# Order of work in a two-transformer kernel: output projections by chunks inside the attentions, rotations at another place, last pieces by halves, another order at the head

## What is computed

```python
def first_block(x, ...):
    for i in range(2):
        h = x @ w_in[i]                       # q, k, v, index heads, u, vs
        a_out = dsa_attention(q, k, v, qi, ki, wi)     # 64 selected keys a query
        b_out = spatial_gating(gelu(u), gelu(vs), ...)
        mix = concatenate([a_out, b_out]) @ w_o[i]
        x = layer_norm(ALPHA * x + mix, ...)
        ffn = (silu(gate) * up) @ w_ffn_out[i]         # gate, up = x @ w_ffn_in[i]
        ple = (p[i] @ w_ple[i]) * sigmoid(x @ w_ple_gate[i])
        x = layer_norm(ALPHA * x + ffn + ple, ...)

def second_block(x, c, ...):
    cond = silu(c)
    for layer in range(2):
        sh1, sc1, g1, sh2, sc2, g2 = split(cond @ ada_w[layer] + ada_b[layer], 6)
        h = modulate(rms_norm(x), sh1, sc1)
        # layer 0: latent attention and a dilated one; layer 1: differential and block attention
        y = (even_mixer if layer == 0 else odd_mixer)(h, ...)   # ends in "@ w_out"
        x = x + g1 * y
        h = modulate(rms_norm(x), sh2, sc2)
        x = x + g2 * squared_relu(h @ mlp_w1[layer]) @ mlp_w2[layer]
    return x
```

## Time and profile before

| | us |
|---|---|
| three executions | 1358.96, 1360.89, 1361.48 |
| the profiled execution | 1359.15 |
| its span | 1357.3 |
| PE busy | 1301.2 |
| DVE busy | 919.9 |
| ACT busy | 654.1 |

### The profile page before, as it was taken

How to read it: one execution, slowest core, us unless ns; L and a number is a source line. 1 busy time by engine, 2 the same in 40 slices (tenths; PEclk the granted TensorE clock), 3 DMA queues, 4 the chain that set the end, 5 groups by cost and what they waited for, 6 DMA issues and landing times.

```text
span 1357.3 us, 16066 instructions
## 1 busy us (share of the span) xinstructions
PE 1301.2 (96%) x6436; PEld 1073.8 (79%) x6467; DVE 919.9 (68%) x1233; ACT 654.1 (48%) x882; POOL 114.4 (8%) x145
## 2 busy tenths in 40 slices
PE   5999999999899999999998999999999978999998
PEld 5877888887787788888698977888887767888886
DVE  4867777765695877775769856857667875644444
ACT  4653544443463544444465555544446544644542
POOL 2001000000000100000225200000004410000000
PEclk8999999999999999999999999999999989999999
DMA  9515587774451668886263304876754421445550
GB/s 371 219 48 186 221 312 308 310 304 148 186 179 63 218 247 310 310 310 233 82 202 125 127 1 165 330 282 261 291 222 184 155 94 39 179 175 182 174 182 31
DMA packets 40362, 270.36 MB, mean 199 GB/s; under 512 B 4560, under 2 KB 4560, under 8 KB 12000
## 3 DMA queue, kind: packets, MB, share of 16 engines
q1 hardware_dynamic: 37712, 259.31, 51.6%
q0 software_dynamic: 2432, 8.98, 1.8%
q10 hardware_dynamic: 144, 1.05, 0.2%
HBM read 268.27 MB, written 1.05 MB: 198 GB/s over the span
## 4 chain that ended last, share of the span: by engine, by line
PE 83%; DVE 10%; ACT 2%; issue 2%; DMA 1%; POOL 1%; SPq 0%; DVEq 0%; ACTq 0%; POOLq 0%
PE ps L1468 48%; PE ps L1458 24%; PE ps L1482 5%; DVE WB L1776 3%; PE ps L1442 2%; PE ps L1567 2%; PE ps L1543 1%; DMA RAW<-W 1%; ACT E L1580 1%; DVE st L2052 1%; ACT WB L1580 1%; DVE st L1980 1%; POOL st L1390 0%; DVE st L2129 0%; DVE X L2097 0%
## 5 line engine op out<-in xcount | busy, mean ns | idle before, releaser
L1776 DVE TENSOR_TENSOR WB<-RAW,WB 128x2048 fp32r<-128x2048 f32 (+4 forms) x210 | 453.5, 2162 | 271.5 <-ACT WB L1580 270.8
L1580 ACT ACTIVATE WB<-RAW 128x2048 fp32r<-128x2048 f32 (+4 forms) x210 | 379.9, 1810 | 210.5 <-PE ps L1468 199.6
L1458 PE MATMUL ps<-WB,XTH 128*128 128x512 f32 (+3 forms) x1176 | 314.4, 389 | 13.0 <-ACT XTH L1580 13.0
L1468 PE MATMUL ps<-WB,XTH 128*128 128x512 f32 (+3 forms) x1176 | 304.6, 381 | 3.4 <-DVE WB L1776 3.3
L1468 PE MATMUL ps<-WB,XTL 128*128 128x512 f32 (+3 forms) x1176 | 304.0, 380 | 1.1 <-DVE XTL L1781 1.1
L1458 PEld LDWEIGHTS ps<-WB,XTH 128*128 128x128 f32 x1176 | 215.0, 190 | 49.2 <-ACT XTH L1580 13.4
L1468 PEld LDWEIGHTS ps<-WB,XTH 128*128 128x128 f32 x1176 | 219.1, 190 | 43.5 <-DVE WB L1776 5.5
L1468 PEld LDWEIGHTS ps<-WB,XTL 128*128 128x128 f32 x1176 | 219.1, 190 | 39.5 <-DVE XTL L1781 1.3
L1458 PE MATMUL ps<-WB,HTH 128*128 128x512 f32 (+1 forms) x452 | 124.4, 396 | 0.5 <-ACT HTH L1580 0.5
L1468 PE MATMUL ps<-WB,HTH 128*128 128x512 f32 (+1 forms) x452 | 123.9, 395 | 0.0
L1468 PE MATMUL ps<-WB,HTL 128*128 128x512 f32 (+1 forms) x452 | 123.8, 394 | 0.0
(11 more groups left out here) (173 smaller groups left out, 964.8 us busy)
## 6 DMA issues: line engine op xcount, KB each, us to landing
RAW<-W SPq DMA_DIRECT2D x220, 1024.0 KB, 4.9
RAW<-W SPq DMA_DIRECT2D x22, 768.0 KB, 4.3
VEC<-vecd POOLq DMA_DIRECT2D x10, 512.0 KB, 7.7
RAW<-W SPq DMA_DIRECT2D x8, 512.0 KB, 3.4
RAW<-W SPq DMA_DIRECT2D x4, 648.0 KB, 5.3
RAW<-W SPq DMA_DIRECT2D x4, 576.0 KB, 3.9
GB<-xTd ACTq DMA_DIRECT2D x1, 1024.0 KB, 7.4
X<-xd SPq DMA_DIRECT2D x1, 1024.0 KB, 17.5
```

Of the source, the lines that this page charges most:

```text
L1458: eng.matmul(banks[b][:, 0:cw], x2[j][0], hi[:, j, c0:c0 + cw], start=first and j == 0, stop=False)
L1468: op = eng.matmul(banks[b][:, 0:cw], x2[j][0 if low_w else 1], (lo if low_w else hi)[:, j, c0:c0 + cw], start=False, stop=last and end and ...
L1580: return eng.activation(dst, src, f, **k)
L1776: eng.tensor_tensor(WB[:, it["raw"], 0:w], RAW[:, it["raw"], 0:w], WB[:, it["high"], 0:w].bitcast(F32), ALU.subtract).then_inc(*up("wl", n))
```

## The change

Eleven bf16 products and a memset are added, twelve padding products taken away, and some steps cut into smaller ones; all else is the same work in another order.

- **Head.** `xT` comes as three transfers (four quarters of the split `x0`), the constants in two, of which the larger part and the small vectors are asked for only after the input is split; the first chunk's items hold 2, 3 and 3 blocks (`FIRST`) instead of 4 and 4; the load of `x` comes four loads later; eleven products on a constant of ones (`warm`) stand at the very start of TensorE's queue; the `silu` of `cond` moves behind the sine and cosine.
- **Output projections.** `linear_k` does the first chunk by items: the blocks that are ready early for both t inside the attention, the others when their block of `MIX` is normalised, with four (or two) transposes directly ahead of their products. The guard and its flag go.
- **Attention.** `between[k]` puts the rotations after scores(k), so between VectorE's maxima and the step that needs the exponentials. Low parts are put down only in steps k < n-2, no longer in the last ones.
- **Halves.** `partial` does t's last products by column halves c, and `last(t, c, done)` is called for each; the last results are stored as four transfers of 128x512.
- **Layer 0 to 1 of the first block.** `mid_at=2` puts the transposes of t = 1 behind the first item of the second chunk; the two `rope_sel` steps stand together.

```diff
+FIRST = [(0, 2), (2, 3), (5, 3)]
...
+        def linear_k(name, lhs, evac, ready, turned=False):
+            its = chunk_items(name)
+            w, g, ps = its[0]["w"], uid(), [take(), take()]
+            advance()
+            its = its[::-1] if turned else its
+            for it in its:
+                for t in range(2):
+                    yield from ready(it["a"], t)
+                    b, fr = ps[t]
+                    lows([it])
+                    do("mm", it, t, "x", [(b, 0, w, (g, t) if it is its[-1] else None)], it is its[0], it is its[-1],
+                       wanted(lhs[t], "x", it), fr if it is its[0] else [], 0, it is its[-1], t)
...
                 old = list(low)
+                if k < len(between):
+                    for f in between[k]:
+                        f()
                 if 1 <= k <= n:
                     turns(units[k - 1], pads[k - 1] if k <= len(pads) else 2)
...
-                lows(old)
+                if k < n - 2:
+                    lows(old)
                 if k >= 2:
                     values(units[k - 2])
             cur["lag"] = False
-            lows()
...
-        loads(3)
-        do("load_x")
+        do("warm", free[0][0])
+        loads(2)
+        do("load_x1")
+        do("x0", 0, 0)
         advance(1)
-        xt_w = [[("xl0", t)] for t in range(2)]
-        do("x0", 0)
+        do("x0", 0, 4)
+        advance(1)
+        do("x0", 1, 0)
+        do("x0", 1, 4)
         advance()
-        do("x0", 1)
-        do("setup")
+        do("load_rest")
...
+            def ready(a, t):
+                if a == 0:
+                    while "out" not in keys_[t]:
+                        yield
+                    mo[t].extend(to_XT(MIX, 4, [keys_[t]["out"]], t, pad=3 if t else 0))
+
             def out_start():
-                while "out" not in keys_[0]:
-                    yield
-                mo[0][:] = to_XT(MIX, 8, [keys_[0]["out"], sgo], 0)
+                for t in range(2):
+                    mo[t].extend(to_XT(MIX, 8, [sgo], t, base=4))
                 yield
-                yield from linear("w_o", "x", mo, put_o(0), touter=True, guard=lambda: tail["go"], pad=(0, 3),
-                                  mid=lambda: mo[1].extend(to_XT(MIX, 8, [keys_[1]["out"], sgo], 1, pad=3)))
+                yield from linear_k("w_o", mo, put_o(0), ready, turned=True)
...
-            def last(t, done):
-                for c in range(2):
-                    do("add_out", (i, t, c), t, c, acc4[t][c][0], [done[c]] + x_o[t])
-                    give(acc4[t][c][0], ("add_out", (i, t, c)))
+            def last(t, c, done):
+                do("add_out", (i, t, c), t, c, acc4[t][c][0], [done] + x_o[t])
+                give(acc4[t][c][0], ("add_out", (i, t, c)))
+                if c == 0:
+                    return
...
-                fill = lined(part((2, 5)), [
-                    None, [ch[3, 1][1], ch[4, 1][0]], None,
-                    [ch[4, 0][1]], None,
-                    [ch[4, 1][1]], None,
-                    [lambda: turn_qk(3, 0, 8, twm), lambda: turn_qk(3, 1, 8, twm)],
-                    [lambda: turn_qk(4, 0, 12, twm), lambda: turn_qk(4, 1, 12, twm)]])
+                ch[4, 1][0]()
+                fill = part((2, 5))
+                between = [[ch[3, 1][1]], [ch[4, 0][1]], [ch[4, 1][1]],
+                           [lambda: turn_qk(3, 0, 8, twm), lambda: turn_qk(3, 1, 8, twm)],
+                           [lambda: turn_qk(4, 0, 12, twm), lambda: turn_qk(4, 1, 12, twm)]]
...
+            def warm(b):
+                on.wait_ge(*at("ones", 0))
+                for _ in range(11):
+                    op = eng.matmul(banks[b][:, :], cstb[:, 0:128], cstb[:, 128:640], start=True, stop=True)
+                op.then_inc(*up("warm", 0))
```

190 lines of the change are left out of this document (112 added, 78 removed).

## The result

| | before | after |
|---|---|---|
| median | 1360.83 us (5 executions) | 1354.49 us (5 executions, 1351.83 to 1356.18) |
| ratio | | 0.9946, 95% interval 0.9925 to 0.9966 |
| the profiled execution | 1359.15 us | 1356.18 us |
| its span | 1357.3 us | 1354.4 us |

A forecast was written before the change was run, and what follows sets the result against it. TensorE, busy 1301.2 of 1357.3 us, was taken as the bound, so only its waits and half-clock work could shrink. Terms -5.7, -0.56, -1.65, -3.55, -1.1, -0.6, -1.9 sum to -15.1: from 1359.15 to 1344.0 us, range 1336 to 1353.

The forecast's parts named there:

- Head: Start of the kernel: smaller first transfers let TensorE start at 6.3 instead of 9.69; -5.7 us, bounds -3 and -9.
- rival (c): Head's data come late, with more, smaller transfers in flight on three queues: head -3, total 1346.8 us; chance 0.10.
- rival (d): Clock stays at 1.2 GHz through the head: 1356.4 us, chance 0.06; uncovered copies drop it too: 1363, chance 0.06.
- First block's attentions: First block's two attentions: shorter wait for the low part, against uncovered copies to `XTH`; -0.28 us each, -0.56 for both.
- step 3: Second block's even layer: shorter waits for exponentials and `MIX`, copies to `XTH` uncovered once; -1.65 us, bounds -3 and 0.
- a wait for `XTH` above 1.5: Sign that the prediction is wrong; waits of 0.6 to 0.9 for `XTH` were expected at the ends of attentions.
- Odd layer, first attention: Rotations moved between maxima and `differ` bring E 3.5 earlier, where TensorE waited 6.86; -5.2 us.
- Odd layer, second attention: Low parts between first maxima +2.3 us, two uncovered `XTH` copies +1.15, low part ahead of the last reciprocal gone -1.8.
- step 4: Odd layer, both attentions: rotations, low parts, `XTH` copies and last reciprocal together; net -3.55 us, bounds -7 and 0.
- Boundaries: Layer 0 to 1 of the first block -1.1 us; layer 1 to second block -0.6, from the hidden half residual add.
- End: Kernel's end: 1.37 instead of 2.74 of VectorE behind the last product, smaller last store; -1.9 us, bounds -1.3 and -2.2.
- Rival (b): Attentions give nothing, each new wait eating what the old one gives back; 2 to 4 fall to 0: 1349.9 us; chance 0.20.

The follow-up runs named there:

- e8: e1's kernel without the eleven products on ones at the start of TensorE's queue: 1347.25 us.
- e3: Changed kernel with the even layer's filler products of the early blocks put in attention steps 4 and 5 instead of 1 and 2: 1359.8 us.
- e1: Changed kernel with the even output projection's first chunk done as before the change, the odd one still by items: 1348.2 us.
- e4: e3's kernel with the two transposes of t = 0's attended blocks one attention step ahead of their products: 1356.6 us.
- e7: e1's kernel with the odd layer's rotations put back among the filler's steps: 1353.8 us.
- e6: e1's kernel with low parts of the odd layer's first attention put down in all steps and at its end, as before the change: 1344.41 us.
- e10: e6's kernel with the odd layer's four transposes of t = 0 one attention step ahead of their products: 1342.18 us.
- e9: Changed kernel with both second-block output projections' first chunks and the low parts of the odd layer's first attention as before the change: 1341.28 us.
- e2: Changed kernel with the odd output projection's first chunk done as before the change, the even one still by items: 1357.3 us.
- e12: The changed kernel run again unedited, on the chip of e9 and e10: 1356.04 us (1351.54 to 1359.18).

## Why the prediction was wrong

**Head: right.** -5.99 against -5.7. The first product came 0.5 late, a wait of 1.49 before the second piece was not foreseen, and the waits at the second chunk were 1.3 smaller in sum (1.6 for 2.9); these nearly cancel. Both lags are ScalarE's waits for the input, so rival (c), late data, shows here, small. One stretch at half clock of 3.4 us, as taken, stands in the clock's record of the head in nine of the thirteen traces with the new head, none in the others. The rival (d), a clock down through the whole head, did not come, and e8, at half pace until 15.3, shows that so much of it need not cost anything: the second chunk's high part is what its end waits for.

**First block's attentions: mis-sized, near nothing.** +0.11 instead of -0.28. I had counted one uncovered copy to `XTH` for each attention; there are two, one for each t, 0.69 each. The wait for `MIX` shrank as told, from 1.44 to 0.38.

**Even layer: wrong, and most of the miss.** +7.26 instead of -1.65, 8.9 us. The step that failed is step 3, in two of its terms, with its bound of 0 above. First, "the copies to `XTH` are uncovered once (+0.6)" was mis-sized: the waits were 2.34 and 0.47, 2.2 more. The rows that it was priced from show ScalarE idle, and the end of an attention; inside an attention ScalarE's queue has exponentials and a copy ahead, as the row at 802.12 of the kernel before could have told. The prediction itself had named a wait for `XTH` above 1.5 as a sign of being wrong. Second, and larger, step 3 put at nothing what is left bare once the 24 early products have moved: 1.06 and 1.17 ahead of scores, 1.35 more ahead of the normalised output, 3.6 together. "Eight transposes fall into the first" took them as filler besides; e3 shows that their copies lie on the chain of that wait. A stretch at half clock came with it, 1.7, also without a term. These make 7.5 of the 8.9; the rest is 1.0 of busy time that stays open and the -0.4 for fewer blocks, which does not show apart. e1 shows that the chunk by items causes all of it, e4 the part for the 2.34, e3 that the bare places move with the products. That the wait for the normalised output grew because results of the first chunk now come later for t = 0 and a low part stands between them is read from the order and not tested.

**Odd layer, first attention: right.** -6.53, between the -5.2 taken and the -6.9 without a clock drop; none stands here now. Counted from the part's first scores, E comes 4.1 us earlier (34.26 for 38.32), 3.5 forecast. The wait for it was 1.22, less than the 3.5 written down as its sign, since TensorE also reaches it 1.6 later, with eight transposes more ahead. One reading was wrong: the stretch of 6.83 us at half clock did not cost 3.4, since TensorE was busy for only 3.47 us of it, so about 1.7. e7 confirms the cause.

**Odd layer, second attention: half right.** +4.40 instead of +1.65. The low part between maxima was +2.2 (forecast 2.3, e6 confirms it), the wait for `MIX` -1.89 (forecast -1.8). The two copies cost 1.76 and 0.69 instead of 1.15 together, again the same mis-sized term, and a stretch at half clock of 3.4 us stands there, for which step 4 had no term; TensorE was busy for 2.85 of it, so it cost 1.4. These add to 4.2. e10 confirms the first copy, e9 both together.

**Boundaries: one right, one wrong.** -0.96 against -1.1 from layer 0 to 1. From layer 1 to the second block nothing instead of -0.6: the wait ahead of the transposes of the normalised X is as it was (0.71 for 0.72), so the half of the residual add that is done earlier was not on the path.

**End: right in kind.** -1.46 from the last landmark instead of -1.9. The 1.37 on VectorE (1.41) and the 0.6 of the smaller store came as told, but 0.5 was lost ahead of them: before, VectorE could start on the first column half 11.08 behind the last landmark, while the last products still ran, and now it starts on the second one 11.55 behind it.

**Rivals.** Rival (b), that the attentions give nothing, was nearest in kind: the attentions' sum was +5.3 in this execution (0.11, 0.09, 7.26, -6.53 and 4.40). That the median of 1354.49 lies nearer to (d)'s 1356.4 is chance. The range ended at 1353 since (b) took "nothing" as its worst; nothing was not the bound, as eight uncovered places could each cost more than the wait that they replace. Rival (d) had a half-clock stretch behind uncovered copies at the right price, 1.7 or a little less each, and two came in the second block, but it was tied to a clock that fails in the head.

## What to carry to other kernels

A copy on an in-order engine costs what stands ahead of it in that engine's queue, so the wait of a transpose followed at once by its product is priced from a row with the same queue, not from one where the copying engine was idle; one step of the pipeline between them took the wait away here. That did not yet make the other order worth it: in the odd layer the old order stayed 1.2 us faster by the traces. Work that fills one bare place has to be looked for at the place it leaves. And a step held back from one phase, here a low part, turns up in the next, where it may stand ahead of something that is waited for.

## What the runs showed of the hardware

TensorE's granted clock fell to half for stretches of 3.4, 6.8 or 10.2 us during or soon behind waits, and not alike each time: in the same stretch of the dilated attention two kernels with the same order there had 3.4 us (changed kernel, 54.3 us in all) and 10.2 us (e2, 57.2 us in all). Executions of one kernel differ too, with mean granted clocks from 0.991 to 0.999 (e12). This spread, 1351.54 to 1359.18 for one kernel, is wider than several of the parts that were to be told apart, and comparing the same landmark in two traces was the way around it.

A program without products at its start worked at the half-clock pace until about 15.3 us (e8), where the window showed 1.00. The length of equal products is the better witness there: 1.01 us for three at half pace, 0.60 at full.
